# A two-block layer on one core: the second block's columns taken from rows without their norm, the norm applied at the evictions, the last norm's weights multiplied in ahead

## The chip, the cores and the metric

The kernel runs on one core of a Trainium2 chip. The metric is the device time of one execution in microseconds. "Before" was timed three times; the median was 762.43 us (762.39 to 763.29).

## The reference, cut to what matters

A layer of two blocks over 256 tokens of width 1024. The first block ends in a mixture of 16 experts and a norm; the second begins with a norm of its own:

```
h = h + g2 * hier_moe(u2, ...)                 # experts' sum, gated, added to the residual
x = rmsnorm(h, norm_final_g)                   # end of block one: h * r1 * gain
xn = rmsnorm_2(x, norm_gain)                   # start of block two: x * r * norm_gain
proj = xn @ w_in
aq, ak, av, ag, bq, bf, bi, bg, gate_a, gate_b = split(proj)
kb, qb, vb = sigmoid(-bf), silu(bq), bi        # decay f = sigmoid(bf)
ya = attention(norm(aq), norm(ak), av) * silu(ag) @ w_up_a
yb = norm(recurrence(qb, kb, vb, f)) * silu(bg) @ w_up_b
out = x + (sigmoid(gate_a) * ya + sigmoid(gate_b) * yb) @ w_out   # then one more gated term
```

Both norms scale a row by one number per token. With r2 the product of the two norms' factors, `xn @ w_in` is `((h * gain) * norm_gain) @ w_in`, each row times r2, so r2 can be applied before the product or after it.

## The kernel before, in words

**Weights.** All weights stream through one list of pieces (`PIECES`, 1024 columns by 128 partitions, 512 KB each) with a ring of eight slots in `T.raw`, loaded by the SyncE queue as each slot comes free. Products are made in three passes of fp32r: ScalarE copies a piece to its high part (`his`, line 1416, a ring of five slots `T.hi`), VectorE subtracts it to get the low part in place (`lows_to`, line 1859), and TensorE multiplies high by high, low by high and high by low (`mm3`, lines 596 to 598). A piece of block two is 24 products of 256 columns when the weights stand still (`turned=True`: `bq`, `bf`) and 12 of 512 columns otherwise.

**Order.** Nothing schedules the engines but the order in which each one's program is written out by hand; waits are on semaphores. `his(n)` and `lows_to(i)` say how far each engine has come in the list of pieces, and stand between the other work.

**End of the experts.** After expert 15, `rows_back(s, c)` brings the sums of slot chunk s, columns half c, back to token order with a product by a 0/1 matrix (lines 1154 and 1155; four products of 512 columns each call). It accumulates over s in banks `PZ[2:4]` for c = 0 and `PM` for c = 1. The last chunk's own sums come out of `down(15, ...)`, and `rows_out(2, c)` splits them (ScalarE line 1714, VectorE line 2412).

**The join.** `gy` multiplies the banks by the gate g2 (line 2437), `add_gy` adds the residual `T.X` (line 2442), `final_gain` multiplies by the last norm's weights into `T.X3` (line 2448). GpSimd does one of the four quarters of the latter two (lines 542 and 545). ScalarE sums the squares of `T.X` and of `T.X3` (line 1623; one sum on VectorE, line 2455), VectorE makes the combined mean (lines 2460 to 2464), GpSimd takes the power -1/2 (`r2`, line 547), and VectorE scales the rows, `T.X4 = T.X3 * r2` (line 2470). TensorE then turns `T.X4` in four groups of four 128x128 blocks (`u3_cols`, line 654), ScalarE and VectorE make high and low parts of the columns times `norm_gain` (`cols_scaled`: lines 1449, 1450 and 1887, 1889; into `T.Ah`, `T.Al`), and the chunk `bq` begins.

```
u3_cols(0), u3_cols(2)
uses("bq", 0, 1, A, u3, turned=True)
u3_cols(4)
uses("bq", 1, 2, A, u3, turned=True)
u3_cols(6)
uses("bq", 2, 4, A, u3, turned=True)
```

**After it.** `bq` gets a silu into `T.T1`, `bf` two sigmoids into `T.T2` and `T.fA` (ScalarE line 1761, straight from the banks). Then come eight levels of the recurrence: per level VectorE does a low part, a `decay_step` (line 2513), a query product (line 2490) and two masked copies (line 2505), while TensorE does one piece of `bi` or `aq` and one `level` (line 1249). The other chunks are copied or activated from their banks.

## Time and profile before

| | |
|---|---|
| median of the runs | 762.43 us (762.39 to 763.29) |
| profiled execution, its own time | 763.19 us |
| its span in the profile | 761.9 us |
| TensorE matmul busy | 715.5 us (94% of the span) |
| VectorE busy | 498.1 us (65%) |
| ScalarE busy | 377.3 us (50%) |
| GpSimd busy | 118.1 us (16%) |
| mean granted TensorE clock | 0.983 |

The span is what the trace holds; the execution's own time has 1.29 us more around it. Places in the trace are in microseconds from the span's start: the experts end at about 502, the columns of block two start after that, and the levels of the recurrence run from about 545 to 584.

### The profile page before, as it was taken

The numbers are of one execution on the slowest core, as the hardware profiler recorded it, in microseconds if no ns is written. First come the engines' busy times: TensorE is split into PE (matmuls) and PEld (weight loads), VectorE is DVE, ScalarE is ACT, GpSimd is POOL, SyncE is SP. The second block draws the span as 40 slices with busy tenths as digits, with TensorE's granted clock in tenths as the row PEclk, the third lists the DMA queues.
The fourth block names the chain that finished last, engine by engine and source line by source line (L and its number), as shares of the span: only waits on it lengthen the run. The fifth ranks groups of instructions, "written<-read, shape, count | busy, mean of one in ns | idle before, by whom it ended". The sixth has DMA issues, their size and how long they took to land.

```text
span 761.9 us, 9899 instructions
## 1 busy us (share of the span) xinstructions
PE 715.5 (94%) x3764; PEld 575.4 (76%) x3764; DVE 498.1 (65%) x716; ACT 377.3 (50%) x547; POOL 118.1 (16%) x86
## 2 busy tenths in 40 slices
...
GB/s 318 361 295 373 256 320 220 249 227 243 110 140 225 336 101 56 240 147 192 185 243 339 361 367 367 360 70 92 173 114 121 178 216 160 165 139 185 174 139 56
DMA packets 100670, 164.07 MB, mean 215 GB/s; under 512 B 10768, under 2 KB 45293, under 8 KB 100494
## 3 DMA queue, kind: packets, MB, share of 16 engines
...
HBM read 162.33 MB, written 1.08 MB: 214 GB/s over the span
## 4 chain that ended last, share of the span: by engine, by line
PE 79%; DVE 11%; ACT 3%; POOL 2%; DMA 2%; issue 1%; SPq 1%; ACTq 0%; DVEq 0%
PE p L596 22%; PE p L598 21%; PE p L597 21%; DVE s_rawr L1859 4%; PE p L665 2%; PE p L654 2%; PE p L700 1%; PE p L724 1%; DMA s_ZC<-in_w_ada_dram 1%; ACT s_hi L1416 1%; PE p L1249 1%; POOL s_BI L486 1%; PE p L712 1%; PE p L1129 1%; DVE s_L L2513 0%
## 5 line engine op out<-in xcount | busy, mean ns | idle before, releaser
L1859 DVE TENSOR_TENSOR s_rawr<-s_raw,s_hi 128x1024 fp32r<-128x1024 f32 x223 | 273.7, 1258 | 59.1 <-ACT s_hi L1416 58.6
L1416 ACT ACTIVATE s_hi<-s_raw 128x1024 fp32r<-128x1024 f32 x240 | 243.7, 1054 | 69.7 <-PE p L598 41.0
L596 PE MATMUL p<-s_hi,s_Ah 128*128 128x512 f32 (+1 forms) x464 | 186.7, 402 | 2.1 <-POOL s_rawr L467 1.0
L598 PE MATMUL p<-s_hi,s_Al 128*128 128x512 f32 (+1 forms) x464 | 179.7, 387 | 0.0
L597 PE MATMUL p<-s_rawr,s_Ah 128*128 128x512 f32 (+1 forms) x464 | 179.4, 387 | 0.0
L596 PEld LDWEIGHTS p<-s_hi,s_Ah 128*128 128x128 f32 x464 | 87.2, 188 | 28.7 <-issue 7.8
L598 PEld LDWEIGHTS p<-s_hi,s_Al 128*128 128x128 f32 x464 | 87.1, 188 | 18.4
L597 PEld LDWEIGHTS p<-s_rawr,s_Ah 128*128 128x128 f32 x464 | 87.4, 188 | 15.7 <-issue 0.2
L596 PE MATMUL p<-s_hi,s_Bh 128*128 128x512 f32 x192 | 77.0, 401 | 2.7 <-DVE s_rawr L1859 2.7
L597 PE MATMUL p<-s_rawr,s_Bh 128*128 128x512 f32 x192 | 75.5, 393 | 0.0
L598 PE MATMUL p<-s_hi,s_Bl 128*128 128x512 f32 x192 | 75.5, 393 | 0.0
L467 POOL TENSOR_TENSOR s_rawr<-s_raw,s_hi 128x1024 fp32r<-128x1024 f32 x17 | 43.9, 2592 | 70.4 <-ACT s_hi L1416 70.3
L596 PE MATMUL p<-s_Ah,s_hi 128*128 128x256 f32 x128 | 38.7, 302 | 7.0 <-DVE s_Al L1878 4.0
L596 PEld LDWEIGHTS p<-s_hi,s_Bh 128*128 128x128 f32 x192 | 36.4, 190 | 10.3 <-issue 2.7
L596 PE MATMUL p<-s_hi,s_Ch 128*128 128x512 f32 x104 | 42.3, 406 | 0.4 <-DVE s_rawr L1859 0.2
L598 PEld LDWEIGHTS p<-s_hi,s_Bl 128*128 128x128 f32 x192 | 36.5, 190 | 7.9
L597 PEld LDWEIGHTS p<-s_rawr,s_Bh 128*128 128x128 f32 x192 | 36.5, 190 | 7.2
L598 PE MATMUL p<-s_hi,s_Cl 128*128 128x512 f32 x104 | 40.6, 390 | 0.0
L597 PE MATMUL p<-s_rawr,s_Ch 128*128 128x512 f32 x104 | 40.6, 390 | 0.0
L597 PE MATMUL p<-s_Al,s_hi 128*128 128x256 f32 x128 | 37.8, 295 | 0.0
L598 PE MATMUL p<-s_Ah,s_rawr 128*128 128x256 f32 x128 | 37.6, 294 | 0.0
L596 PEld LDWEIGHTS p<-s_Ah,s_hi 128*128 128x128 f32 x128 | 26.2, 205 | 9.3 <-issue 5.1
(358 smaller groups left out, 877.2 us busy)
## 6 DMA issues: line engine op xcount, KB each, us to landing
...
s_GS<-in_w_ada_dram SPq DMA_DIRECT2D x16, 1024.0 KB, 7.6
...
```

Of the source, the lines that this page charges most:

```text
L467: pool.tensor_tensor(T.lo[:, i % NRAW, :], T.raw[:, i % NRAW, :], T.hi[:, i % NHL, :].bitcast(F32), ALU.subtract).then_inc(*S.lo_pool(i))
L486: pool.tensor_tensor(bv, bv, T.sc[:, tt, 0:ns].unsqueeze(1).broadcast_to([128, 8, ns]), ALU.add).then_inc(*S.pool_dsa("mask", tt))
L596: pe.matmul(o, xh, wh, start=start, stop=False)
L597: pe.matmul(o, xh, wl, start=False, stop=False)
L598: return pe.matmul(o, xl, wh, start=False, stop=stop)
L654: r = pe.transpose(PT[b][:, 256 * k + 128 * tt:256 * k + 128 * tt + 128], src(tt, k0 + k), ident)
L665: r = pe.matmul(bank[32 * j:32 * j + 32, :], T.CS[:, 4 * h + j, :], w[:, j, :], start=h == 0, stop=h == 1, tile_position=(0, 32 * j))
L700: r = pe.matmul(PM[h % 2][:, 256 * (j // 2):256 * (j // 2) + ns], qT[o:o + 64, h // 2, 128 * tt:128 * tt + 128], kT(h, ns), start=True, st ...
L712: r = pe.transpose(PT[b][:, c:c + 128], Lv[:, per * g + j, 128 * s:128 * s + 128], ident)
L724: r = pe.matmul(PM[0][:, 64 * h:64 * h + 64], Pv[:, h, 128 * s:128 * s + 128], v(h, s), start=s == 0, stop=s == tt)
L1416: act.activation(T.hi[:, i % NHL, :], T.raw[:, i % NRAW, :], ACT.Copy).then_inc(*S.hi(i))
L1859: dve.tensor_tensor(T.lo[:, i % NRAW, :], T.raw[:, i % NRAW, :], T.hi[:, i % NHL, :].bitcast(F32), ALU.subtract).then_inc(*S.lo_dve(i))
```

## The change

- **Experts' sums back by halves.** `rows_back` is called for column half 0 of chunks 0 and 1 ahead of `down(15)`, and for half 1 of those chunks behind `rows_back(2, 0)`.
- **Weights of the last norm ahead.** While expert 2 runs, VectorE multiplies g2 by the last norm's weights (`T.gated`) and the residual by them (`T.X3`), three instructions of 128x1024. At the join `rows_in` makes one product by `T.gated` and one addition for each quarter, which gives `h * gain` in `T.X3` at once. `residual` makes `T.X` (the sum without the weights, needed for the first norm's mean) from the same banks later, between the low parts. GpSimd has no part of it, and its `memset` of `T.fS` waits for the last `rows_back` instead of the scaled rows.
- **Columns from unnormalised rows.** `T.X4` is gone; `u3_cols` turns `T.X3` itself, the first two groups as soon as its first half is there. The eight sums of squares stand on ScalarE behind the columns' high parts; the mean, `r2` and `r1` follow between the pieces of `bf`.
- **The evictions apply the norm.** For chunks with tokens on the partitions, `r2` is the scale of the ScalarE activation or of a VectorE `tensor_scalar` (`copy_normed`, `silu_normed`, `gate_second`). For `bq` and `bf`, whose tokens lie along the free dimension, TensorE spreads `r2` over the partitions with two transposes in the middle of `bf` (`norm`), VectorE copies it to `T.r2row` and multiplies the banks by it (`normed`, four instructions), and ScalarE's silu and sigmoids then read SBUF. The two sigmoids of `bf` change places: `fA` is made first, then `T2` in place.
- `his` and `lows_to` are placed anew: the parts of `bq` 0 and 1 come ahead of `rows_out(2, ...)`.

```diff
@@ names @@
-    T.X4 = T.YR[:, :].rearrange("p (t d) -> p t d", t=2)
+    T.gain, T.gated = T.BI[:, 1024:2048], T.YR[:, 0:1024]
+    T.r1, T.r2, T.r2row = T.st[:, 500:502], T.st[:, 506:508], T.sg[:, 0, :]
@@ pool_program @@
-    q.wait_ge(*S.dve_moe.at("gy", 0, 1))
-    pool.tensor_tensor(T.X[:, 1, 0:512], T.X[:, 1, 0:512], T.ZC[0][:, 1, :], ALU.add).then_inc(*S.pool_moe("x"))
-    pool.tensor_tensor(T.X3[:, 1, 0:512], T.X[:, 1, 0:512], T.BI[:, 1024:1536], ALU.mult).then_inc(*S.pool_moe("x3"))
+    q.wait_ge(*S.pe_rows.at(2, 1))
+    pool.memset(T.fS, 1.0).then_inc(*S.pool_hgrn("S", 0))
     q.wait_ge(*S.dve_moe.at("norm2"))
-    pool.tensor_tensor(st[:, 506:508], st[:, 504:506], T.mhalf[:, 0:2], ALU.pow).then_inc(*S.pool_moe("r2"))
+    pool.tensor_tensor(T.r2, st[:, 504:506], T.mhalf[:, 0:2], ALU.pow).then_inc(*S.pool_moe("r2"))
     rstd(S.pool_moe, ("r1",), 500, 496, 2, 1024.0, 1e-6)
-    q.wait_ge(*S.dve_moe.at("x4", 3))
-    q.wait_ge(*S.act_moe.at("sq3", 1, 1))
-    pool.memset(T.fS, 1.0).then_inc(*S.pool_hgrn("S", 0))
@@ pe_program @@
-    for s in range(2):
-        rows_back(s, 0), rows_back(s, 1)
+    rows_back(0, 0), rows_back(1, 0)
     q.wait_ge(*S.dve_moe.at("lo", 15))
     for c in range(2):
         down(15, 0, (c,), None)
         down(15, 1, (c,), ("dn15", c, 1))
-    rows_back(2, 0), rows_back(2, 1)
+    rows_back(2, 0)
+    rows_back(0, 1), rows_back(1, 1), rows_back(2, 1)
     m_free[0] = m_free[1] = S.dve_moe.at("gy", 1, 1)
-    for z in range(4):
-        z_free[z] = [S.dve_moe.at("gy", 0, 1)]
+    z_free[0] = z_free[1] = [S.dve_rows.at("lo", 2, 1)]
+    z_free[2] = z_free[3] = [S.dve_moe.at("gy", 0, 1)]
     t_free[0] = t_free[1] = S.dve_moe.at("lo", 15)
     def u3_cols(k0):
-        q.wait_ge(*S.dve_moe.at("x4", 3 if k0 > 2 else 1))
-        turn(lambda tt, k: T.X4[:, tt, 128 * k:128 * k + 128], ("u3", k0), S.dve_cols.at("u3", k0))
+        q.wait_ge(*S.dve_moe.at("x3", k0 // 4, 1))
+        turn(lambda tt, k: T.X3[:, tt, 128 * k:128 * k + 128], ("u3", k0), S.dve_cols.at("u3", k0))
     def u3(h):
         return "u3", 2 * h
...
     uses("bq", 1, 2, A, u3, turned=True)
     u3_cols(6)
     uses("bq", 2, 4, A, u3, turned=True)
-    chunk_freed("bq", S.act_hgrn.at("bq", 0), S.act_hgrn.at("bq", 1))
-    uses("bf", 0, 4, A, u3, turned=True)
-    chunk_freed("bf", S.act_hgrn.at("f", 0), S.act_hgrn.at("f", 1))
+    chunk_freed("bq", S.dve_hgrn.at("bq", 0), S.dve_hgrn.at("bq", 1))
+    uses("bf", 0, 2, A, u3, turned=True)
+    b = turn_bank("norm")
+    q.wait_ge(*S.pool_moe.at("r2"))
+    for tt in range(2):
+        r = pe.transpose(PT[b][:, 128 * tt:128 * tt + 128], T.r2[:, tt:tt + 1].broadcast_to([128, 128]), ident)
+    r.then_inc(*S.turned("norm", 0))
+    t_free[b] = S.dve_moe.at("norm row")
+    uses("bf", 2, 4, A, u3, turned=True)
+    chunk_freed("bf", S.dve_hgrn.at("bf", 0), S.dve_hgrn.at("bf", 1))
@@ act_program @@
+    his_to(AT["bq", 2])
     rows_out(2, 0), rows_out(2, 1)
-    junk = T.L[:, :].rearrange("p (t d) -> p t d", t=2)
-    q.wait_ge(*S.dve_moe.at("x", 0, 0))
-    squares(S.act_moe, ("sq",), T.X, T.X4, 488, 0, 0)
...
-    squares(S.act_moe, ("sq3",), T.X3, junk, 492, 1, 1)
+    def sums(key, src, junk, c, n, tt):
+        q.wait_ge(*S.dve_moe.at(key, n, tt))
+        squares(S.act_moe, ("sq " + key,), src, junk, c, n, tt)
+    cols_scaled("u3", 0, T.Ah, T.g_in2), cols_scaled("u3", 2, T.Ah, T.g_in2)
+    his(1)
+    cols_scaled("u3", 4, T.Ah, T.g_in2)
+    his(1)
+    cols_scaled("u3", 6, T.Ah, T.g_in2)
+    his(1)
+    for n in range(2):
+        for tt in range(2):
+            sums("x3", T.X3, T.RGS, 492, n, tt)
+    his(1)
+    for n in range(2):
+        for tt in range(2):
+            sums("x", T.X, T.GS[:, 0, :, :], 488, n, tt)
     his(2)
-    cols_scaled("u3", 0, T.Ah, T.g_in2), cols_scaled("u3", 2, T.Ah, T.g_in2)
-    q.wait_ge(*S.pool_moe.at("r1"))
-    for tt in range(2):
-        act.activation(T.X[:, tt, :], T.X3[:, tt, :], ACT.Copy, scale=st[:, 500 + tt:501 + tt]).then_inc(*S.act_moe("xf", tt))
-    his(2)
-    cols_scaled("u3", 4, T.Ah, T.g_in2)
-    his(1)
-    cols_scaled("u3", 6, T.Ah, T.g_in2)
-    his(2)
-    def heads(key, name, dst, fn, sc):
+    def heads(key, ready, src, dst, fn, sc):
         for i in range(2):
...
+            q.wait_ge(*S.dve_hgrn.at(ready, i))
+            act.activation(dst[:, 2 * i:2 * i + 2, :], src[:, 2 * i:2 * i + 2, :], fn, scale=sc).then_inc(*S.act_hgrn(key, i))
+    def copy_normed(name, dst, bank):
+        q.wait_ge(*S.piece.at(name, 3, 0))
+        act.activation(dst, bank[:, :], ACT.Copy, scale=T.r2[:, 0:1]).then_inc(*S.act_copy(name))
...
-    heads("bq", "bq", T.T1, ACT.Silu, 1.0)
+    q.wait_ge(*S.pool_moe.at("r1"))
+    for tt in range(2):
+        q.wait_ge(*S.act_moe.at("sq x", 1, tt))
+        act.activation(T.X[:, tt, :], T.X3[:, tt, :], ACT.Copy, scale=T.r1[:, tt:tt + 1]).then_inc(*S.act_moe("xf", tt))
+    his(1)
+    heads("bq", "bq", T.T1, T.T1, ACT.Silu, 1.0)
+    his(2)
+    heads("f", "bf", T.T2, T.fA, ACT.Sigmoid, 1.0)
+    q.wait_ge(*S.act_hgrn.at("f", 1))
+    heads("bf", "bf", T.T2, T.T2, ACT.Sigmoid, -1.0)
+    his_to(AT["aq", 3])
+    copy_normed("bi", T.BV[:, 0, :], banks("bi")[0])
     his(4)
-    heads("bf", "bf", T.T2, ACT.Sigmoid, -1.0)
-    heads("f", "bf", T.fA, ACT.Sigmoid, 1.0)
-    his(4)
-    copy("bi", T.BV[:, 0, :], banks("bi")[0])
-    his(4)
-    copy("aq", T.ZC[0][:, 0, :], banks("aq")[0])
+    copy_normed("aq", T.ZC[0][:, 0, :], banks("aq")[0])
@@ dve_program @@
+        if n == 2:
+            dve.tensor_tensor(T.gated, T.G2[:, :], T.gain, ALU.mult).then_inc(*S.dve_moe("gated gain"))
+            for tt in range(2):
+                dve.tensor_tensor(T.X3[:, tt, :], T.X[:, tt, :], T.gain, ALU.mult).then_inc(*S.dve_moe("gained"))
...
+    lows_to(AT["bq", 2])
     rows_out(2, 0), rows_out(2, 1)
-    def gy(n):
-        for tt in range(2):
-            q.wait_ge(*S.pe_rows.at(2, n))
-            q.wait_ge(*S.dve_ada.at(11))
-            dve.tensor_tensor(T.ZC[n][:, tt, :], T.G2[:, 512 * n:512 * n + 512], out_bank(T, n, tt)[:, :], ALU.mult).then_inc(*S.dve_moe("gy", n, tt))
-    def add_gy(n, tt):
+    def rows_in(n, tt):
         c = slice(512 * n, 512 * n + 512)
+        q.wait_ge(*S.pe_rows.at(2, n))
+        q.wait_ge(*S.dve_moe.at("gained"))
+        dve.tensor_tensor(T.ZC[n][:, tt, :], T.gated[:, c], out_bank(T, n, tt)[:, :], ALU.mult).then_inc(*S.dve_moe("gated", n, tt))
+        q.wait_ge(*S.dve_moe.at("gated", n, tt))
+        dve.tensor_tensor(T.X3[:, tt, c], T.X3[:, tt, c], T.ZC[n][:, tt, :], ALU.add).then_inc(*S.dve_moe("x3", n, tt))
+    def residual(n, tt):
+        c = slice(512 * n, 512 * n + 512)
+        q.wait_ge(*S.dve_moe.at("x3", n, tt))
+        dve.tensor_tensor(T.ZC[n][:, tt, :], T.G2[:, c], out_bank(T, n, tt)[:, :], ALU.mult).then_inc(*S.dve_moe("gy", n, tt))
         q.wait_ge(*S.dve_moe.at("gy", n, tt))
         dve.tensor_tensor(T.X[:, tt, c], T.X[:, tt, c], T.ZC[n][:, tt, :], ALU.add).then_inc(*S.dve_moe("x", n, tt))
-    def final_gain(n, tt):
-        c = slice(512 * n, 512 * n + 512)
-        q.wait_ge(*S.final_gain_in.at(0))
-        q.wait_ge(*S.dve_moe.at("x", n, tt))
-        dve.tensor_tensor(T.X3[:, tt, c], T.X[:, tt, c], T.BI[:, 1024:2048][:, c], ALU.mult).then_inc(*S.dve_moe("x3", n, tt))
-    gy(0)
-    add_gy(0, 0), final_gain(0, 0)
-    gy(1)
-    add_gy(1, 0), add_gy(1, 1)
-    final_gain(1, 0), final_gain(1, 1)
-    dve.scalar_tensor_tensor(out=T.X4[:, 0, 512:1024], in0=T.X[:, 0, 512:1024], scalar=1.0, in1=T.X[:, 0, 512:1024], op0=ALU.mult, op1=ALU.mult,
-                             accum_out=st[:, 490:491]).then_inc(*S.dve_moe("sq"))
+    rows_in(0, 0), rows_in(0, 1)
+    rows_in(1, 0)
+    cols_scaled("u3", 0, T.Ah, T.Al, T.g_in2)
+    rows_in(1, 1)
+    cols_scaled("u3", 2, T.Ah, T.Al, T.g_in2)
+    lows_to(AT["bq", 3])
+    cols_scaled("u3", 4, T.Ah, T.Al, T.g_in2)
+    lows_to(AT["bf", 0])
+    cols_scaled("u3", 6, T.Ah, T.Al, T.g_in2)
+    residual(0, 0), residual(0, 1)
+    lows_to(AT["bf", 1])
+    residual(1, 0), residual(1, 1)
+    lows_to(AT["bf", 2])
     v = st[:, 488:496].rearrange("p (s n t) -> p s n t", s=2, n=2)
-    q.wait_ge(*S.act_moe.at("sq3", 1, 1))
-    q.wait_ge(*S.dve_moe.at("sq"))
+    q.wait_ge(*S.act_moe.at("sq x", 1, 1))
     dve.tensor_tensor(st[:, 496:500].rearrange("p (s t) -> p s t", s=2), v[:, :, 0, :], v[:, :, 1, :], ALU.add).then_inc(*S.dve_moe("sum"))
     q.wait_ge(*S.dve_moe.at("sum"))
     dve.tensor_scalar(st[:, 502:504], st[:, 496:498], 1e-6 / 1024.0, 1e-12, ALU.mult, ALU.add).then_inc(*S.dve_moe("norm1"))
     q.wait_ge(*S.dve_moe.at("norm1"))
     dve.scalar_tensor_tensor(out=st[:, 504:506], in0=st[:, 498:500], scalar=1.0 / 1024.0, in1=st[:, 502:504],
                              op0=ALU.mult, op1=ALU.add).then_inc(*S.dve_moe("norm2"))
-    q.wait_ge(*S.pool_moe.at("r2"))
-    for n in range(2):
-        for tt in range(2):
-            c = slice(512 * n, 512 * n + 512)
-            dve.tensor_scalar(T.X4[:, tt, c], T.X3[:, tt, c], st[:, 506 + tt:507 + tt], None, ALU.mult).then_inc(*S.dve_moe("x4", 2 * n + tt))
-    cols_scaled("u3", 0, T.Ah, T.Al, T.g_in2), cols_scaled("u3", 2, T.Ah, T.Al, T.g_in2)
-    lows_to(AT["bf", 0])
-    cols_scaled("u3", 4, T.Ah, T.Al, T.g_in2)
-    lows_to(AT["bf", 1])
-    cols_scaled("u3", 6, T.Ah, T.Al, T.g_in2)
+    lows_to(AT["bf", 3])
+    def normed(name, dst):
+        for i in range(2):
+            q.wait_ge(*S.piece.at(name, 3, i))
+            dve.tensor_tensor(dst[:, 2 * i:2 * i + 2, :], banks(name)[i][:, :].rearrange("p (k t) -> p k t", k=2),
+                              T.r2row.unsqueeze(1).broadcast_to([128, 2, 256]), ALU.mult).then_inc(*S.dve_hgrn(name, i))
+    def copy_normed(name, dst, bank):
+        q.wait_ge(*S.piece.at(name, 3, 1))
+        dve.tensor_scalar(dst, bank[:, :], T.r2[:, 1:2], None, ALU.mult).then_inc(*S.dve_copy(name))
+    q.wait_ge(*S.turned.at("norm", 0))
+    dve.tensor_copy(T.r2row, T.PT[T.turn_bank["norm",]][:, 0:256]).then_inc(*S.dve_moe("norm row"))
+    q.wait_ge(*S.dve_moe.at("norm row"))
+    normed("bq", T.T1)
+    lows_to(AT["bi", 2])
+    normed("bf", T.T2)
```

## Rows read from the trace of the kernel before

**Rows 1.** The page's busy time of each engine over the span.
```profile
PE 715.5 (94%) x3764; PEld 575.4 (76%) x3764; DVE 498.1 (65%) x716; ACT 377.3 (50%) x547; POOL 118.1 (16%) x86
```
**Rows 2.** Waits of TensorE, longest first: total, times, longest.
```profile
PE p L654 <- DVE s_YR L2470: 9.6, 1, 9.6
PE p L665 <- DMA s_GS<-in_w_ada_dram: 7.1, 2, 6.3
```
**Rows 3.** Stretches: length, busy time of PE, PEld, DVE, ACT, POOL, clock, DMA.
```profile
502.00:516.50 14.50, 2.00 (x9) 1.57 (x8) 11.43 (x23) 10.47 (x23) 6.48 (x6) 0.57 0.14 52
521.20:545.30 24.10, 24.10 (x192) 23.61 (x192) 10.15 (x11) 14.16 (x20) 1.53 (x1) 1.00 0.59 168
545.30:583.80 38.50, 38.11 (x229) 32.47 (x228) 38.15 (x44) 8.75 (x10) 23.98 (x14) 1.00 0.39 115
```
**Rows 4.** The chain that ended last, at the join: start, length, what.
```profile
500.71 1.28 DVE s_ZC L2437 x2
...
509.91 0.72 POOL s_st L547
...
516.53 0.58 PE p L596
```
**Rows 5.** Timeline of TensorE: start, length, line, operands [idle before].
```profile
492.80 0.48 PE L1154 MATMUL p<-s_Lr,s_GSr 128*128 128x512 f32 x1
...
496.54 0.39 PE L596 MATMUL p<-s_hi,s_Ch 128*128 128x512 f32 x1
...
521.88 0.36 PE L596 MATMUL p<-s_Ah,s_hi 128*128 128x256 f32 x1
...
524.84 0.60 PE L654 MATMUL p<-s_blob,s_YR 128*128 128x128 f32 x4
525.20 0.36 PE L596 MATMUL p<-s_Ah,s_hi 128*128 128x256 f32 x1
```
**Rows 6.** Timeline of ScalarE and VectorE around the join and columns.
```profile
498.10 0.60 ACT L1714 ACTIVATE s_Lr<-p 128x512 fp32r<-128x512 f32 x1 [4.64 <-PE p L598]
...
501.91 0.68 DVE L2442 TENSOR_TENSOR s_X<-s_X,s_ZC 128x512 f32<-128x512 f32 x1
...
502.70 1.57 DVE L2448 TENSOR_TENSOR s_PP<-s_X,s_BI 128x512 f32<-128x512 f32 x1
...
525.48 0.47 ACT L1449 ACTIVATE s_Ah<-p,s_VC 128x256 fp32r<-128x256 f32 x1 [1.52 <-PE p L654]
...
526.35 0.48 DVE L1887 SCALAR_TENSOR_TENSOR s_Al<-p,s_VC,s_Ah 128x256 fp32r<-128x256 f32 x1 [1.14 <-ACT s_Ah L1450]
```
**Rows 7.** Timeline of VectorE and TensorE between experts 2 and 3.
```profile
374.65 4.63 DVE L1859 TENSOR_TENSOR s_rawr<-s_raw,s_hi 128x1024 fp32r<-128x1024 f32 x4 [0.26 <-ACT s_hi L1416]
...
386.52 0.60 PE L1129 MATMUL p<-s_blob,s_hid 128*128 128x128 f32 x4
...
387.79 0.69 DVE L2407 TENSOR_TENSOR s_Cl<-p,s_Ch 128x512 fp32r<-128x512 f32 x1 [4.13 <-ACT s_Ch L1707]
```
**Rows 8.** Timeline of ScalarE and VectorE between `bf` and the levels.
```profile
538.13 1.28 ACT L1761 ACT_TABLE_LOAD   x1
...
542.75 0.60 ACT L1761 ACTIVATE s_T<-p 128x512 f32<-128x512 f32 x1 [0.84 <-PE p L598]
543.25 1.08 ACT L1761 ACTIVATE s_L<-p 128x512 f32<-128x512 f32 x2
544.20 2.02 ACT L1416 ACTIVATE s_hi<-s_raw 128x1024 fp32r<-128x1024 f32 x2
...
545.30 1.23 DVE L1859 TENSOR_TENSOR s_rawr<-s_raw,s_hi 128x1024 fp32r<-128x1024 f32 x1 [5.93 <-ACT s_hi L1416]
...
587.80 0.69 DVE L2537 TENSOR_TENSOR s_ZC<-s_ZC,s_st 128x512 f32<-128x512 f32 x1
```
**Rows 9.** Pauses of TensorE and the granted clock (the last number but two).
```profile
122.00:128.00 6.00, 4.58 (x30) 3.22 (x28) 0.76 (x2) 2.34 (x2) 4.08 (x2) 1.00 0.95 350
...
315.56 0.47 PE L596 MATMUL p<-s_hi,s_Bh 128*128 128x512 f32 x1 [2.53 <-DVE s_rawr L1859]
...
316.40:319.80 3.40, 3.40 (x10) 2.63 (x9) 3.07 (x4) 3.07 (x5) 0.00 (x0) 0.50 1.08 358
...
504.00:506.00 2.00, 0.00 (x0) 0.00 (x0) 2.00 (x5) 1.66 (x6) 1.40 (x1) 0.53 0.04 16
```

More of the change, by code:

```diff
@@ L1504, in gate_second @@
             q.wait_ge(*S.piece.at(name, 3, tt))
-            act.activation(T.GS[:, w, tt, 512 * n:512 * n + 512], banks(name)[tt][:, :], ACT.Sigmoid).then_inc(*S.act_gate(name, tt))
+            act.activation(T.GS[:, w, tt, 512 * n:512 * n + 512], banks(name)[tt][:, :], ACT.Sigmoid, scale=T.r2[:, tt:tt + 1]).then_inc(*S.act_gate(name, tt))
     def turn_ret(name, k0, dst):
@@ L1755, in act_program, with silu_normed @@
     cols_scaled("u3", 6, T.Ah, T.g_in2)
+    his(1)
[6 more added lines that the diff above has]
+            sums("x", T.X, T.GS[:, 0, :, :], 488, n, tt)
     his(2)
-    def heads(key, name, dst, fn, sc):
+    def heads(key, ready, src, dst, fn, sc):
         for i in range(2):
-            q.wait_ge(*S.piece.at(name, 3, i))
-            act.activation(dst[:, 2 * i:2 * i + 2, :], banks(name)[i][:, :].rearrange("p (k t) -> p k t", k=2), fn, scale=sc).then_inc(*S.act_hgrn(key, i))
+            q.wait_ge(*S.dve_hgrn.at(ready, i))
[3 more added lines that the diff above has]
+        act.activation(dst, bank[:, :], ACT.Copy, scale=T.r2[:, 0:1]).then_inc(*S.act_copy(name))
+    def silu_normed(name, dst):
+        for tt in range(2):
+            q.wait_ge(*S.piece.at(name, 3, tt))
+            act.activation(dst(tt), banks(name)[tt][:, :], ACT.Silu, scale=T.r2[:, tt:tt + 1]).then_inc(*S.act_moba(name, tt))
     def head_squares(name, z):
@@ L1791, in act_program @@
     his(1)
-    copy("ak", T.ZC[1][:, 0, :], banks("ak")[0])
+    copy_normed("ak", T.ZC[1][:, 0, :], banks("ak")[0])
     head_squares("ak", T.ZC[1])
@@ L1796, in act_program @@
     his(2)
-    gate_silu(S.act_moba, "bg", lambda tt: T.RGS[:, 0, 512 * tt:512 * tt + 512], ())
+    silu_normed("bg", lambda tt: T.RGS[:, 0, 512 * tt:512 * tt + 512])
     his(2)
@@ L1800, in act_program @@
     his(2)
-    copy("av", T.AV[:, 0, :], banks("av")[0])
+    copy_normed("av", T.AV[:, 0, :], banks("av")[0])
     his(3)
@@ L1804, in act_program @@
     his(1)
-    gate_silu(S.act_moba, "ag", lambda tt: T.RGS[:, 1, 512 * tt:512 * tt + 512], ())
+    silu_normed("ag", lambda tt: T.RGS[:, 1, 512 * tt:512 * tt + 512])
     his(2)
@@ L2425, in dve_program @@
         lows_to(AT[f"up{n + 2}", 2] if n < 14 else AT["dn15", 1] + 1)
+        if n == 2:
+            q.wait_ge(*S.final_gain_in.at(0))
+            q.wait_ge(*S.dve_ada.at(11))
+            q.wait_ge(*S.dve_gather.at("rows", 1))
+            dve.tensor_tensor(T.gated, T.G2[:, :], T.gain, ALU.mult).then_inc(*S.dve_moe("gated gain"))
+            for tt in range(2):
+                dve.tensor_tensor(T.X3[:, tt, :], T.X[:, tt, :], T.gain, ALU.mult).then_inc(*S.dve_moe("gained"))
         if n == 0:
@@ L2525, in dve_program @@
         if lv == 3:
-            copy("bi", T.BV[:, 1, :], banks("bi")[1])
+            copy_normed("bi", T.BV[:, 1, :], banks("bi")[1])
     def head_sums(name, c):
@@ L2548, in out_norm @@
                           st[:, 104 + 4 * tt:108 + 4 * tt].unsqueeze(2).broadcast_to([128, 4, 128]), ALU.mult).then_inc(*S.dve_hgrn("yb", tt))
-    copy("aq", T.ZC[0][:, 1, :], banks("aq")[1])
+    copy_normed("aq", T.ZC[0][:, 1, :], banks("aq")[1])
     head_sums("aq", 112)
```

16 lines of the change are left out of this document (2 added, 14 removed).

## The prediction

> **What bounds the kernel now.** The page's first part says that TensorE is busy 94% of the span [rows 1], so only two things can move the time: products taken out, which this change does not do, or stretches in which TensorE waits or runs at the lower clock. The waits of TensorE, read second, put one on top: 9.6 us, once, before the transposes at line 654, for line 2470, the scaled rows [rows 2]. The stretches, read third, show what surrounds it: from 502.0 to 516.5 TensorE is busy 2.0 us of 14.5 at a mean clock of 0.57, while VectorE has 11.4 and ScalarE 10.5 [rows 3]. The chain that ended last goes through the same place without TensorE: gates at 500.71, the power on GpSimd at 509.91, the first product of `bq` at 516.53 [rows 4]. So the change acts where an idle stretch of about 14 us lies, plus what the lower clock costs behind it. The next stretches say where a gain can be lost: from 521.2 to 545.3 TensorE is never idle and VectorE has 10 of 24 us, but from 545.3 to 583.8 VectorE is busy 38.15 of 38.5 us and TensorE 38.11 [rows 3]. The levels are bound by both.
>
> **The unit costs.** Products of 512 columns: sixteen from 492.80 to 496.54, 0.234 each. Products of 256: a piece of `bq` with four transposes behind it goes from 521.88 to 525.20, 3.32 us, of which the transposes are about 0.45, so 2.88 for the 24 products (0.12 each) [rows 5]. ScalarE: 0.60 for 128x512, 0.47 for 128x256 (two in a row 0.85, from 525.48 to VectorE's start); VectorE: 0.68 for 128x512 (0.60 when the next one does not depend on it), 0.48 for 128x256 (two in a row 0.88); hand-over between engines 0.03 to 0.05 [rows 6].
>
> **The change step by step.** Times are places in the trace of before.
>
> *Expert 2.* Three VectorE instructions of 128x1024, 3 x 1.15 = 3.5 (four parts of that size took 4.63 [rows 7]), stand between four low parts and expert 3's hidden values. They end at 382.8, the hidden values at 383.6, the next two low parts at 384.8 and 386.0. TensorE takes the hidden values at 386.52 and VectorE was idle 4.13 us ahead of 387.79 [rows 7]. Cost nothing; the cover left is 2.1 us, and with no cover it would be 3.5.
>
> *Sums back by halves.* Ahead of `down(15)` stand 8 products instead of 16, so `down` starts 1.87 earlier, at 494.67, and its first half is done at 496.2. Before, ScalarE got it at 498.10 [rows 6]. Split on both engines: 497.56 and 498.92. TensorE does `rows_back(2, 0)` at 497.6, the eight postponed products over the wait for the second half, and ends at 501.3; VectorE has half 0 at 498.84. The parts of `bq` 0 and 1, now ahead of the split, fall into 493.5 to 496.9, where both engines stood idle (4.64 us on ScalarE [rows 6]), so they cost nothing.
>
> *Rows.* Each quarter is now one product and one addition, 0.70 + 0.60, done at 500.23 and 501.54 for half 0. TensorE turns these at 501.57 and is through with eight transposes at 502.5. ScalarE's high parts 502.25 to 503.10, VectorE's low parts to 504.01 (it does the third quarter in between, done at 503.00, so the two meet). `bq` starts at 504.04; before, 516.53 [rows 4].
>
> *`bq`.* Four pieces of 2.88 and two more groups of transposes of 0.45: to 516.46. Every input is there in time, by the order of VectorE: columns 2 at 506.1 against 507.4, columns 4 at 509.4 against 510.7, columns 6 at 512.7 against 513.6, the low part of `bq` 3 at 510.8 against 513.6. So the second piece of `bq` starts at 507.4 instead of 521.88 [rows 5]: 14.5 us earlier, 12.5 from the pause and 2 from the first piece at the full clock.
>
> *`bf`: what is given back.* Behind columns 6 VectorE has the four `residual` pairs, 4 x 1.30, and two low parts of 1.15. The low part of `bf` 0 is done at 516.48, just in time; that of `bf` 1 at 520.25, against TensorE at 519.39: a wait of 0.9. The two transposes that spread `r2` cost 0.25. `r2` itself: last square on ScalarE 519.85, three small sums 0.6, the power 0.72 [rows 4], so 521.6; TensorE comes to it at 523.16, and 1.6 us of cover are left. Behind them VectorE has the copy of the row (0.45) and `bq` times the row (1.3), then the low part of `bf` 3, done at 526.60 against 526.3: 0.3. So `bf` ends at 529.5; together 1.5 us given back.
>
> *Into the levels.* VectorE multiplies the last half of `bf` behind the low part of `bi` 1: done at 530.87. ScalarE then has four sigmoids in which the second pair waits for the first, to 532.80 (its table load, 1.28 [rows 8], ends at 530.57 and costs 0.3), and the high part of `bi` 3, so VectorE starts the low part of `bi` 3 at 533.79. Before, the sigmoids ran straight from the banks, the last two from 543.25, and that instruction stands at 545.30, with 5.93 us of idle VectorE ahead of it [rows 8], and from it on VectorE is never idle until 583.8 [rows 3]; the new list of the levels is the same. So the gain that reaches the levels is the shift of this instruction. The same working applied to the order of before puts it at 545.64, so it runs 0.34 late, and like is subtracted from like: 11.85 us. TensorE by itself would have gained 12.75 there; 0.9 stays in waits of the levels.
>
> *What the trace of before does not show.* The product of a bank with a row spread over an outer dimension: nearest row 0.69 for a product with a spread operand, line 2537 [rows 8]; below, no less than that; above, the 1.57 of line 2448 [rows 6]. The nearer row is taken; three such instructions lie on the path, so at most 2.7 later. Activations and `tensor_scalar` with a scale per partition: like the columns of before, nothing. GpSimd's `memset` (0.95) now runs at 501.6, beside VectorE's additions: between 0 and 0.7, since 0.2 of 0.9 would be slack; 0.2 taken. For a contention of this kind there is a row: line 2448 took 1.57 instead of 0.68 while GpSimd worked [rows 6]. The Trainium skill (GPSIMD Engine Reference, section 1) says that GpSimd shares its SBUF interfaces with VectorE and collides with instructions of two SBUF inputs; the trace agrees (1.57), and by the rule the removal of GpSimd's quarters would help too, which the working above already has in its 0.68.
>
> **The sum.** 763.19 - 11.85 + 0.2 = 751.5 in the profiled execution's own time. That execution stood 0.76 above the median of the runs shown, so 750.8. No products leave, and only the two transposes of `r2` come; behind the levels everything shifts as it is.
>
> **The rivals.**
>
> *A, the forecast:* 750.8, its own range 749.7 to 752.0. Chance 0.54.
>
> *B, the clock falls all the same.* TensorE has a pause from 501.3 to 504.0 with 0.9 us of transposes in it. After 2.53 us of idling ahead of 315.56 the clock went to half from 316.4 to 319.8, 3.4 us long; after a pause of 1.4 us in the stretch at 122 it stayed at 1.00; before the change it fell at 504.1, two microseconds after the last product [rows 9]. 2.7 with transposes inside lies between. It would cost half of 3.4, 1.3 to 1.7: 752.3. Chance 0.25. The Trainium skill (TensorE: Matmul & The Clock Gate, Part 4) says that transposes do not count as activity for the clock; by this rule the pause is a whole 2.7, longer than the one that cost it at 315, and B is the likelier of the two; by the rows alone it is open.
>
> *C, VectorE and ScalarE are slower between `bf` 1 and the sigmoids* (spread operand, or one more part that comes late where I count covers of 0 to 0.3): 1.5 to 2.7 later, 752.3 to 753.5. For: the order there has three places without slack. Chance 0.11.
>
> *D, expert 2 pays:* the cover of 2.1 is gone and TensorE waits up to 3.5: 754.3. Against: 4.13 us of idling. Chance 0.03.
>
> *E, it does not do what it says:* the levels or the loads take the gain back, 762.4. Against: DMA share 0.39 and 0.59 behind the join [rows 3]. Chance 0.03.
>
> *F, slower:* the wait moves into the middle of `bf`. TensorE's queue is in order, and everything behind the spreading of `r2` waits for the last square. It decides from the point where `r2` is more than 12 + 1.6 = 13.6 us later than worked out; each microsecond beyond costs one. At 16 late, 765. For it: eight squares and four pairs are queued between the parts. Against: they take 10 us together. Chance 0.04.
>
> **How the numbers follow.** The range holds A with its own range, B and most of C: 749.3 (the low end is TensorE's own gain of 12.75, and 0.3 for the working's error) to 753.6. What a measurement can tell from no change is about 0.2%, 1.5 us: A to D are faster, 0.93; E is the same, 0.03; F slower, 0.04.
>
> **What would show it.** In the profile after: line 654's wait of 9.6 gone, and a pause of about 1.6 before `bq`; no stretch at half clock near 504 (B if there is one); `bq` near 504 and the levels' first VectorE part near 533.8; a wait of TensorE near 0.9 before `bf` 1 and 0.3 before `bf` 3; the VectorE products of `normed` at 0.68. A wait of TensorE at the two `norm` transposes, or at expert 3, would make it wrong, as would a chain in the levels that starts later than 535.5.

## The result, and the profile after

The changed kernel takes 756.6 us (median of four runs, 755.82 to 757.94). The kernel before, timed beside it, takes 762.86 (762.39 to 763.34). The ratio is 0.992, with a 95% interval of 0.9903 to 0.9937. So the change gains 6.3 us. The prediction had said 750.8 with a range from 749.3 to 753.6: it had the direction, and nearly twice the size. The profiled execution took 756.98 in its own time, its span was 755.7, and its mean granted clock 0.993.

First the page's busy times, beside [rows 1]:

```profile
PE 715.3 (95%) x3766; PEld 573.9 (76%) x3766; DVE 507.0 (67%) x724; ACT 378.5 (50%) x549; POOL 114.6 (15%) x84
```

TensorE's busy time is the same to 0.2 us. What changed is how long it waits. Its three longest waits in the part of the change, in the changed kernel (total, times, longest):

```profile
PE p L1253 <- DVE s_BI L2538: 1.6, 3, 1.0
PE p L592 <- DVE s_Al L1902: 1.5, 1, 1.5
PE p L650 <- DVE s_PP L2461: 1.4, 1, 1.4
```

The 9.6 us ahead of the transposes [rows 2] are gone, and so is a wait of 3.0 ahead of `bq`, which [rows 2] does not list:

```profile
516.53 0.58 PE L596 MATMUL p<-s_Ah,s_hi 128*128 128x256 f32 x1 [2.97 <-DVE s_rawr L1859]
```

A wait of 1.4 ahead of the transposes and one of 1.5 ahead of `bq` stand in their place. The second was forecast, the first was not. In the levels (line 1253) the waits are 1.6, and another 0.2 is for ScalarE's sigmoid; before they were 0.4 together, and the prediction let 0.9 stay there. The stretches of the changed kernel (length, busy time of PE, PEld, DVE, ACT, POOL, clock, DMA) stand beside those of [rows 3]:

```profile
502.00:516.50 14.50, 11.50 (x78) 10.77 (x79) 10.10 (x18) 5.23 (x11) 0.95 (x1) 0.88 0.23 64
506.00:508.00 2.00, 0.71 (x3) 0.74 (x4) 1.70 (x4) 1.91 (x4) 0.00 (x0) 0.76 0.00 0
508.00:510.00 2.00, 2.00 (x12) 2.00 (x11) 2.00 (x4) 0.00 (x0) 0.00 (x0) 0.50 0.03 8
510.00:512.00 2.00, 2.00 (x18) 2.00 (x17) 0.38 (x1) 0.00 (x0) 0.00 (x0) 0.89 0.00 0
```

From 502.0 to 516.5 TensorE is busy 11.50 us instead of 2.00. But the clock still falls: in the second half of 506 to 508 it goes to 0.50, which is 1.2 of 2.4 GHz, and it comes back in 510 to 512. The mean clock of the whole stretch is 0.88, where before it was 0.57.

Now the join itself. The timeline of ScalarE and VectorE in the changed kernel shows what the prediction had not seen:

```profile
497.09 0.60 ACT L1718 ACTIVATE s_Lr<-p 128x512 fp32r<-128x512 f32 x1 [0.94 <-PE p L594]
500.68 0.60 ACT L1718 ACTIVATE s_Lr<-p 128x512 fp32r<-128x512 f32 x1 [3.00 <-PE p L1151]
...
497.72 0.69 DVE L2425 TENSOR_TENSOR s_Lr<-p,s_Lr 128x512 fp32r<-128x512 f32 x1
501.31 0.69 DVE L2425 TENSOR_TENSOR s_Lr<-p,s_Lr 128x512 fp32r<-128x512 f32 x1 [2.90 <-ACT s_Lr L1718]
501.92 0.68 DVE L2459 TENSOR_TENSOR s_ZC<-s_YR,p 128x512 f32<-128x512 f32 x1
```

And TensorE's timeline over the same stretch:

```profile
493.39 0.44 PE L1125 MATMUL p<-s_blob,s_hid 128*128 128x128 f32 x2 [0.70 <-DVE s_hid L2412]
...
498.02 0.39 PE L594 MATMUL p<-s_hi,s_Cl 128*128 128x512 f32 x1
498.47 0.50 PE L1150 MATMUL p<-s_Lr,s_GSr 128*128 128x512 f32 x1
...
500.20 0.39 PE L1151 MATMUL p<-s_Lr,s_GSr 128*128 128x512 f32 x1
...
502.06 0.50 PE L1150 MATMUL p<-s_Lr,s_GSr 128*128 128x512 f32 x1 [0.56 <-DVE s_Lr L2425]
...
504.70 1.09 PE L650 MATMUL p<-s_blob,s_PP 128*128 128x128 f32 x8 [1.45 <-DVE s_PP L2461]
507.29 0.55 PE L592 MATMUL p<-s_Ah,s_hi 128*128 128x256 f32 x1 [1.49 <-DVE s_Al L1902]
```

Read the second row of ScalarE. It is the split of the last chunk's half 1. Its data are the sums of `down(15)`, whose last product starts at 498.02 and takes 0.39, so they are there at 498.41. It starts at 500.68. The bracket names what it waited for: line 1151, the second pass of a `rows_back`. The one that ends there is `rows_back(0, 1)`, whose last product starts at 500.20. The code says why. The split writes its result into `T.Yh[s % 2]`, and for s = 2 that is the place of chunk 0:

```
        if s > 1:
            q.wait_ge(*S.pe_rows.at(s - 2, c))
        act.activation(T.Yh[s % 2][:, 512 * c:512 * c + 512], ...)
```

Before the change, `rows_back(0, 1)` ran ahead of `down(15)`, and this wait was over long before. The change issues it behind `rows_back(2, 0)`, so the wait is live. With a hand-over of 0.04 the split could have started at 498.45: 500.68 - 498.45 = 2.2 us. VectorE's half of the split follows at 501.31, and all of the rows' work stands behind that in VectorE's queue. Half 0 of the rows needed nothing of half 1: its own sums, `rows_back(2, 0)`, were through by about 499.7, yet its first product starts at 501.92.

### The profile page after: what moved, and what is told of

Its sections match the earlier page's. It is cut to its first block, busy times and chain, and to the rows that moved or that the text cites. A ratio compares the mean times of both kernels' runs of the same rounds, so it can differ in the third digit from the quotient of the medians.

```text
span 755.7 us, 9916 instructions
## 1 busy us (share of the span) xinstructions
PE 715.3 (95%) x3766; PEld 573.9 (76%) x3766; DVE 507.0 (67%) x724; ACT 378.5 (50%) x549; POOL 114.6 (15%) x84
## 4 chain that ended last, share of the span: by engine, by line
PE 77%; DVE 12%; ACT 4%; DMA 2%; POOL 2%; issue 2%; SPq 1%; ACTq 0%; POOLq 0%; DVEq 0%
PE p L592 22%; PE p L594 20%; PE p L593 20%; DVE s_rawr L1872 4%; PE p L661 2%; PE p L650 2%; ACT s_hi L1420 2%; DMA s_ZC<-in_w_ada_dram 1%; PE p L696 1%; PE p L720 1%; PE p L1253 1%; POOL s_BI L488 1%; DMA s_raw<-in_w_exp_up_dram 1%; PE p L708 1%; PE p L1125 1%
```

## The experiments

Each ratio below is against the kernel before, timed beside it on the same chip (763.0 for experiments 1 to 4, 762.85 on another chip for 5 to 7). Where a stretch is compared, it runs from the transposes of expert 15 (TensorE, 493.39 in the changed kernel) to the first product of `bf` 1, the first one behind the wait that the prediction put there. This leaves out what differs between executions ahead of it. In the changed kernel it is 524.94 - 493.39 = 31.55 us. In before the transposes of expert 15 stand here:

```profile
492.60 0.44 PE L1129 MATMUL p<-s_blob,s_hid 128*128 128x128 f32 x2 [0.74 <-DVE s_hid L2399]
```

Behind the stretch come the rest of `bf` and the levels. From the eight transposes that follow the last level to the end of the span, all nine profiles have 176.0 to 176.2 us, so nothing behind them makes a difference.

**1. A place of its own for half 1.** The split of (2, 1) goes to a free tile (s_GSr), so it has nobody to wait for. Order and work stay.

```
+    T.Y = lambda s, c: (gs_r[:, 0:512], gs_r[:, 512:1024]) if (s, c) == (2, 1) else ...   # T.Yh, T.Yl
... (the two products of rows_back and both halves of the split take T.Y(s, c))
-        if s > 1:
+        if (s, c) == (2, 0):
             q.wait_ge(*S.pe_rows.at(s - 2, c))
```

> Edit: the split sums of the last slot chunk, column half 1, go to a place of their own, so that ScalarE need not wait until rows_back(0, 1) has read the old one. Everything else is the changed kernel (756.6 us). Theory W (the reordering put a wait for that place in the way: ScalarE's split of half 1 stood at 500.68 behind a product that is only issued after rows_back(2, 0), and VectorE's first gated row stood behind it): the split comes about 2.3 us earlier (near 498.4), the first product of bq near 505.0 instead of 507.3, and the time is 2.0 to 2.3 lower, 754.3 to 754.6; 0.4 to 0.6 more if the lower clock stretch moves off dense work. Rival C (the loss lies in the lower clock and in the levels, the split is covered): under 0.7 lower, 756 or more.

Measured: 752.19 us (751.78 to 752.93), ratio 0.9861 (0.9846 to 0.9877). The intervals of this and of the changed kernel do not touch. It is 4.4 us under the changed kernel, where 2.0 to 2.9 was expected. ScalarE, VectorE and TensorE in its timeline:

```profile
497.29 0.60 ACT L1719 ACTIVATE s_GSr<-p 128x512 fp32r<-128x512 f32 x1 [0.76 <-PE p L595]
...
497.92 0.69 DVE L2426 TENSOR_TENSOR s_GSr<-p,s_GSr 128x512 fp32r<-128x512 f32 x1 [0.67 <-ACT s_GSr L1719]
498.55 0.69 DVE L2460 TENSOR_TENSOR s_ZC<-s_YR,p 128x512 f32<-128x512 f32 x1
...
492.23 0.44 PE L1126 MATMUL p<-s_blob,s_hid 128*128 128x128 f32 x2 [0.70 <-DVE s_hid L2413]
...
501.34 1.09 PE L651 MATMUL p<-s_blob,s_PP 128*128 128x128 f32 x8
503.93 0.36 PE L593 MATMUL p<-s_Ah,s_hi 128*128 128x256 f32 x1 [1.50 <-DVE s_Al L1903]
...
520.18 0.39 PE L593 MATMUL p<-s_Ah,s_hi 128*128 128x256 f32 x1 [0.64 <-DVE s_rawr L1873]
```

The releaser is now the product of `down(15)` itself (line 595). The transposes wait for nothing, `bq` starts at 503.93, where the prediction had said 504.04, and no stretch near it is at the half clock. The stretch is 520.18 - 492.23 = 27.95 us, 3.6 shorter. That settles where most of the miss lies, but not how it divides between the wait and the clock, since both went together.

**2. The halves undone.** `rows_back` is called in the order of before; the rest of the change stays.

```
-    rows_back(0, 0), rows_back(1, 0)
+    for s in range(2):
+        rows_back(s, 0), rows_back(s, 1)
...
-    rows_back(2, 0)
-    rows_back(0, 1), rows_back(1, 1), rows_back(2, 1)
+    rows_back(2, 0), rows_back(2, 1)
```

> Edit: the order of rows_back is that of before (chunks 0 and 1 whole ahead of down(15), chunk 2's halves last); the rest of the change stays. Theory W: the halves' order as built is worth nothing, because what it gives ahead of down(15) (1.9 us) is less than the wait it makes (2.3 us plus the first gated row behind it): bq starts 0 to 1 us earlier than in the changed kernel, time 755.6 to 756.8. Rival C (the halves' order is a gain as forecast, its wait harmless): 1.2 to 1.9 higher, 757.8 to 758.5.

Measured: 755.87 us (754.23 to 757.22), ratio 0.9913 (0.9898 to 0.9927). That is the time of the changed kernel within the intervals. So the halves, as built, bring nothing: what TensorE gains by starting `down(15)` earlier it loses at the shared place. Counted from the transposes of expert 15, `bq` starts after 13.49 us here and after 13.90 in the changed kernel. With a place of their own the halves are worth 755.87 - 752.19 = 3.7 us by the medians, and the intervals do not touch. By the profiles' stretch it is less: here it is 522.15 - 492.41 = 29.74, 1.8 over experiment 1. Of the other 1.9, 1.6 lie between executions: the profiled one, 754.23, is the fastest of the five, and its mean clock is 0.998, where the other four have 0.991 to 0.995. Where the clock fell in those four no profile shows.

**3. The clock alone.** The changed kernel with its wait, but TensorE gets products with no use in its two pauses: five behind the last `rows_back` and six behind the first transposes, into a bank that is overwritten later.

```
+    def fill(n):
+        q.wait_ge(*S.dve_rows.at("lo", 2, 1))
+        for _ in range(n):
+            pe.matmul(PZ[0][:, :], T.PT3[0][:, 0:128], T.Yh[0][:, 0:512], start=True, stop=True)
+    fill(5)
     u3_cols(0), u3_cols(2)
+    fill(6)
```

> Edit: eleven more products of 512 columns into a bank that nobody reads, five in the pause ahead of the first transposes and six in the one ahead of bq; the rest is the changed kernel. They are work that does not count; they only keep TensorE busy for about 2.6 of 2.9 idle us. Theory B (the pause costs a stretch of 3.4 us at half clock in nearly every run, 1.4 us at the levels): no stretch at half clock near 507, time 1.2 to 1.6 lower, 755.0 to 755.4. Rival (the lower clock is absorbed by waits for VectorE behind it): clock back to 1.00 but the time within 0.4 of 756.6. If a product holds up the transposes: up to 0.3 higher.

Measured: 754.02 us (753.16 to 754.53), ratio 0.9884 (0.9868 to 0.99). TensorE's timeline and the stretches of this kernel:

```profile
500.06 0.50 PE L1150 MATMUL p<-s_Lr,s_GSr 128*128 128x512 f32 x1 [0.57 <-DVE s_Lr L2432]
...
501.10 1.30 PE L1220 MATMUL p<-s_Lr,s_GSr 128*128 128x512 f32 x5
502.71 1.09 PE L650 MATMUL p<-s_blob,s_PP 128*128 128x128 f32 x8 [0.31 <-DVE s_PP L2468]
503.56 1.64 PE L1220 MATMUL p<-s_Lr,s_GSr 128*128 128x512 f32 x6
505.30 0.36 PE L592 MATMUL p<-s_Ah,s_hi 128*128 128x256 f32 x1
```

```profile
504.00:506.00 2.00, 1.90 (x12) 1.36 (x11) 1.69 (x4) 1.92 (x4) 0.00 (x0) 1.00 0.00 0
506.00:508.00 2.00, 2.00 (x19) 2.00 (x18) 2.00 (x4) 0.00 (x0) 0.00 (x0) 1.00 0.03 8
```

The wait is as in the changed kernel (0.57 at the last `rows_back`, behind VectorE's split). From the transposes to `bq` it takes 2.59 us in both, so the fillers delay nothing. The clock stays at 1.00, and the stretch is 521.55 - 491.42 = 30.13 instead of 31.55: the clock cost 1.4 us, inside the 1.2 to 1.6 that was expected. By the medians it is 756.6 - 754.02 = 2.6, with intervals that do not touch; the medians hold what the clock does elsewhere too, and the working below goes by the stretch.

**4. Own place and fillers.** Experiment 1 with one and six fillers, so that neither wait nor clock is left.

```
     (own place as in 1)
+    fill(1)
     u3_cols(0), u3_cols(2)
+    fill(6)
```

> Edits of the two together: the own place for half 1 and fillers (one product ahead of the transposes, six ahead of bq). Theory W and B together, additive: 2.2 + 1.4 lower, 753.0. If the pause without the wait no longer costs the clock, B adds nothing: equal to the kernel with the own place alone.

Measured: 752.91 us (751.74 to 753.47), ratio 0.9864 (0.9849 to 0.988), the same as experiment 1. So with the own place in, the fillers add nothing; the 753.0 that was expected of wait and clock together fits both kernels and does not tell them apart. The stretch is 521.34 - 493.40 = 27.94, and experiment 1 had 27.95. Against experiment 3, with the fillers in both, it is 30.13 - 27.94 = 2.2 shorter. That is the wait alone, and it agrees with the 2.2 read from the trace. The medians give 754.02 - 752.91 = 1.1 for it, with intervals that overlap, so by the runs alone this part is not resolved; wait and clock together (4.4 by the medians, 3.6 by the stretch) are.

**5. The same place, another order.** Half 1 keeps the shared place, but `rows_back(0, 1)` goes ahead of `rows_back(2, 0)`, so that it is over sooner. Four products that half 0 doesn't need then stand ahead of it.

```
+    rows_back(0, 1)
     rows_back(2, 0)
-    rows_back(0, 1), rows_back(1, 1), rows_back(2, 1)
+    rows_back(1, 1), rows_back(2, 1)
```

> The changed kernel with rows_back(0, 1) ahead of rows_back(2, 0), no place of its own. Theory W (ScalarE's split of half 1 waits for that product and for nothing else): the split stands about 0.9 us behind the end of down(15) instead of 3.3, the first gated row 1.5 us earlier than in the changed kernel, no fall of the clock, time 752.5 to 753.5. Rival (it is the shared place itself, or the clock has nothing to do with the wait): 755 or more.

Measured: 753.13 us (752.03 to 754.49), ratio 0.9882 (0.9861 to 0.9904). ScalarE and TensorE:

```profile
497.10 0.60 ACT L1719 ACTIVATE s_Lr<-p 128x512 fp32r<-128x512 f32 x1 [1.73 <-PE p L1151]
...
501.12 1.09 PE L650 MATMUL p<-s_blob,s_PP 128*128 128x128 f32 x8 [1.38 <-DVE s_PP L2462]
503.70 0.36 PE L592 MATMUL p<-s_Ah,s_hi 128*128 128x256 f32 x1 [1.49 <-DVE s_Al L1903]
```

The split still waits for line 1151, but 1.73 us instead of 3.00, of which 0.76 are idle for its data anyhow, as in experiment 1. So about 1.0 is left of 2.2, and the wait followed the product that was moved. The stretch says the same: 519.96 - 491.08 = 28.88, 0.9 over experiment 1 and 2.7 under the changed kernel, as the clock did not fall here. The order within the shared place is worth most of it and costs no memory. By the runs the time is as expected (752.5 to 753.5), but the interval just meets that of the changed kernel and overlaps that of experiment 1. Not tried is the other way around the wait, the rows of half 0 ahead of half 1's split in VectorE's program: VectorE stood idle for 2.90 us there.

**6 and 7. The levels.** After experiment 1 the levels' first VectorE part is where it was forecast and the time is still above 750.8. Experiment 6 takes experiment 1 and brings ScalarE's high part of `bi` 3 ahead of the sigmoids, which it stood behind:

```
-    his(2)
+    his(3)
     heads("f", ...)
```

> On top of the kernel with the own place (752.2): ScalarE makes the high part of bi 3 ahead of the sigmoids of bf, not behind them. Theory L (the levels are bound by VectorE's start of them, and VectorE waited 2 us for that high part and then did its low part beside GpSimd in 1.69 us): VectorE's memset ahead of the levels 1.7 us earlier, TensorE's waits of 0.98 and 0.37 in the levels gone, time 1.5 to 2.0 lower, 750.2 to 750.7. Rival (the levels are bound by TensorE, or the sigmoids 1 us later cost as much): within 0.4 of 752.2.

Measured: 752.3 us (751.89 to 752.52), ratio 0.9867 (0.9848 to 0.9885), where 750.2 to 750.7 was expected. Experiment 7 has besides this the low part of `bf` 1 ahead of the last two `residual` pairs, against TensorE's wait there:

```
-    lows_to(AT["bf", 1])
-    residual(1, 0), residual(1, 1)
     lows_to(AT["bf", 2])
+    residual(1, 0), residual(1, 1)
```

> On top of the kernel with bi 3's high part early: VectorE makes the low part of bf 1 ahead of the last two residual pairs. Theory V (TensorE waits 0.65 us for that low part because the pairs stand ahead of it): that wait goes, the mean square comes 1.2 us later and eats most of r2's cover, 0 to 0.6 lower than the kernel it stands on. Rival (r2 is late and TensorE waits at its transposes instead): 0 to 0.5 higher.

Measured: 752.42 us (752.02 to 753.15), ratio 0.9865 (0.9846 to 0.9884). VectorE ahead of the levels, first in experiment 1, then in experiment 6:

```profile
533.53 1.69 DVE L1873 TENSOR_TENSOR s_rawr<-s_raw,s_hi 128x1024 fp32r<-128x1024 f32 x1 [1.99 <-ACT s_hi L1421]
535.28 1.02 DVE L2551 MEMSET s_BI<- 128x512 f32 x2
```

```profile
531.09 2.35 DVE L1873 TENSOR_TENSOR s_rawr<-s_raw,s_hi 128x1024 fp32r<-128x1024 f32 x2
534.43 1.03 DVE L2551 MEMSET s_BI<- 128x512 f32 x2 [0.99 <-ACT s_T L1760]
```

The wait of 1.99 for ScalarE is gone in experiment 6, but TensorE's first level now waits 1.15 us for the sigmoid (at 534.32; in experiment 1 it waited 0.21), since the high part runs ahead of it. From the first product of `bf` 1 to the eighth level the profiles show 567.13 - 520.95 = 46.18 us against 567.52 - 520.18 = 47.34. The trace is 1.2 us shorter there. The medians of the runs are not, and the transposes of expert 15 stand 0.8 later in this profile than in that of experiment 1, so whether the runs gain the 1.2 stays open.

In experiment 7 the wait ahead of `bf` 1 is gone. A small one stands behind the transposes of `r2` instead, and a large one, for the sigmoid, ahead of the first level:

```profile
524.12 0.39 PE L593 MATMUL p<-s_Ah,s_hi 128*128 128x256 f32 x1 [0.39 <-DVE s_rawr L1873]
...
535.66 2.05 PE L1254 MATMUL p<-s_T 128*128 128x128 f32 x16 [2.78 <-ACT s_T L1760]
```

Neither the theory nor its rival had this. The two `residual` pairs come later, so ScalarE's last squares do, and behind them in ScalarE's queue everything to the sigmoids. From the transposes of expert 15 to those behind the last level it takes 82.55 us here, 81.46 in experiment 6 and 82.64 in experiment 1: the edit gives back by the trace what experiment 6 had gained.

## Why the prediction was wrong, point by point

**The failed step.** It is in the part on the sums back by halves: "Split on both engines: 497.56 and 498.92", and with it "VectorE has half 0 at 498.84". The first half was right. Counted from the transposes of expert 15, it was forecast to be split after 497.56 - 492.60 = 4.96 us, and in experiment 1 VectorE has it at 497.25, after 5.02. In the changed kernel it has half 1's split at 502.00, 8.61 after the transposes, where 498.92 - 492.60 = 6.32 was forecast, and it starts on half 0's rows only behind that. For half 1 the working counted its data and the engines, but not whether its place was free. Moving `rows_back(0, 1)` moved its reader behind the writer, and the change keeps the wait that guards this. It measured 2.2 us. With a place of its own (experiment 1) VectorE is through with half 1 after 6.38, and the time, 752.19, lies in the range. An instruction needs its data, its engine and its room; the working asked for the first two.

**The clock, rival B.** It came true in the changed kernel, at its price: 1.4 us against 1.3 to 1.7. But not in the pause that it was argued from. That pause, 2.7 us from the last `rows_back` to `bq` with the eight transposes in it, is in experiment 1, and the clock holds at 1.00 over it, as it does in experiments 6 and 7. In the changed kernel the missed wait made more of it: 0.56 idle, one `rows_back`, then 1.45, the transposes, and 1.49. Experiment 2 has the last three of these (1.47 and 1.49) and experiment 5 nearly so (1.38 and 1.49), and neither profile shows a fall. So the fall was one of six such pauses, and how often it comes in the runs without a profile stays open: their mean clocks are 0.991 to 0.995 for the changed kernel, 0.991 to 0.998 for experiment 2, 0.993 to 0.998 for experiment 5, 0.994 to 0.995 for experiment 1 and 0.995 to 0.998 for experiments 6 and 7. Experiment 4, where no pause is left, has 0.997 to 0.999, but experiment 3 with its filled pauses has 0.992 to 0.998. The Trainium skill (TensorE: Matmul & The Clock Gate, Part 4) says that transposes do not count as activity, so that this pause would be a whole one. The pause of nearly the same length without transposes, 2.4 to 2.6 us, ahead of 315.56 in before [rows 9], cost the clock in five of nine profiles, and this one in none of three; that leans against the rule, on few cases, and settles nothing.

**The levels.** The prediction took the shift of VectorE's low part of `bi` 3 as the gain, since "the new list of the levels is the same". The list is, but not its durations. From this instruction to TensorE's eight transposes behind the last level it is 579.61 - 538.28 = 41.33 us in the changed kernel and 574.87 - 533.53 = 41.34 in experiment 1. The trace of before has these transposes at 585.77, so there it is 585.77 - 545.30 = 40.47, and 0.87 of the gain is given back in both. VectorE and GpSimd of the changed kernel:

```profile
538.28 1.69 DVE L1872 TENSOR_TENSOR s_rawr<-s_raw,s_hi 128x1024 fp32r<-128x1024 f32 x1 [1.99 <-ACT s_hi L1420]
540.03 1.03 DVE L2550 MEMSET s_BI<- 128x512 f32 x2
...
542.78 1.91 DVE L1872 TENSOR_TENSOR s_rawr<-s_raw,s_hi 128x1024 fp32r<-128x1024 f32 x1
```

```profile
537.38 1.51 POOL L560 TENSOR_TENSOR s_GS<-s_T,s_L 128x512 f32<-128x512 f32 x1 [9.84 <-ACT s_T L1759]
542.10 1.51 POOL L570 TENSOR_TENSOR s_L<-s_L 128x512 f32<-128x512 f32 x1 [3.21 <-DVE s_GS L2523]
```

The low part takes 1.69 where it took 1.23 before [rows 8], 0.46 more. GpSimd's product of the first decay, 537.38 to 538.89, runs beside it. In before it ran while VectorE idled, and the next low part is the second line:

```profile
543.43 1.53 POOL L564 TENSOR_TENSOR s_GS<-s_T,s_L 128x512 f32<-128x512 f32 x1 [30.09 <-ACT s_T L1761]
...
549.33 1.58 DVE L1859 TENSOR_TENSOR s_rawr<-s_raw,s_hi 128x1024 fp32r<-128x1024 f32 x1
```

The next low part takes 1.91, and 1.58 in before. GpSimd works beside both; line 570's step lies beside the first for 0.8 us and beside that of before for 0.5. Together 0.46 + 0.33 = 0.8 of the 0.87. For the second of the two no experiment tests the cause. Experiment 6 moved the first overlap. There the low part runs ahead of GpSimd's product and takes half of 2.35, and it is VectorE's own product that meets it, at 1.04 instead of 0.62:

```profile
534.34 1.52 POOL L561 TENSOR_TENSOR s_GS<-s_T,s_L 128x512 f32<-128x512 f32 x1 [10.79 <-ACT s_T L1760]
...
535.38 1.04 DVE L2524 TENSOR_TENSOR s_GS<-s_T,s_L 128x512 f32<-128x512 f32 x1
```

So the price of the first follows whoever stands beside GpSimd's product. VectorE's idle time of 5.93 was thus not all waste: it took in GpSimd's product. The correction "it runs 0.34 late, and like is subtracted from like" was not earned either. Counted from the transposes of expert 15, VectorE's part came 545.30 - 492.60 = 52.70 after them in before, and 533.53 - 492.23 = 41.30 in experiment 1, a gain of 11.40 instead of 11.85.

**Upstream.** The transposes of expert 15 stand at 493.39 against 492.60 before: 0.8 later, and expert 2's added work is not the reason. Experts 2 to 3 take as long as before (372.99 to 387.08 on TensorE, 14.09, as 372.43 to 386.52). The changed kernel and the seven of the experiments have the same code up to there, and in their profiles these transposes stand anywhere from 491.08 to 493.40. Early on the changed kernel's profile is 1.4 behind: a wait that ends at 67.95 in before ends at 69.34 there, and the windows from 26.0 to 29.4 and from 29.4 to 32.4 both have a clock of 0.50, in before 0.53 and 0.96. Some of it comes back behind 316, where the clock fell in before and not in the changed kernel. So it is a difference between executions, and the medians don't carry it as a whole.

**The sum.** Forecast 11.85 of gain. From it come off 0.45 (the 0.34 of the correction and 0.1 of the working), 2.2 for the missed wait, 1.4 for the clock, 0.9 in the levels and 0.8 upstream, which leaves 6.1. The two profiled executions differ by 763.19 - 756.98 = 6.2. The forecast in the profiled execution's time was 751.5, so it missed by 5.4; the wait and the clock, 3.6, are two thirds of that. The prediction had priced the clock as a rival and the wait not at all. The 0.2 for GpSimd's `memset` was not spent: it ran at 503.32 beside VectorE's additions, and these took 0.69, as elsewhere.

**What held.** In experiment 1, `bq` and the low part of `bi` 3 are within 0.3 us of their forecast places, by the trace (503.93 against 504.04; 533.53 against 533.79) and counted from the transposes of expert 15 (11.70 against 11.44; 41.30 against 41.19). A wait ahead of `bf` 1: 0.65, forecast 0.9. The cover of `r2`: it is there at 526.14, and TensorE spreads it at 527.92, so 1.8 are left, forecast 1.6; rival F did not come near. At expert 2 VectorE's idle time is 2.05 ahead of 388.35, forecast 2.1, and rival D did not come. The wait of 0.3 ahead of `bf` 3 is not there. `normed` by a spread operand: two in a row in 1.29, 0.68 for one, the nearer of the two bounds, and rival C was not paid:

```profile
524.94 0.39 PE L592 MATMUL p<-s_Ah,s_hi 128*128 128x256 f32 x1 [0.65 <-DVE s_rawr L1872]
...
527.92 0.38 PE L1229 MATMUL p<-s_blob,s_st 128*128 128x128 f32 x2
```

```profile
528.80 1.29 DVE L2498 TENSOR_TENSOR s_T<-p,s_sg 128x512 f32<-128x512 f32 x2
```

The version to keep is that of experiment 1: 752.2 us, 10.8 less than before on the same chip and 4.4 less than the changed kernel. Experiments 4 to 7 did not beat it by the runs.
